# One encoder layer on one core: the first norm's scale and shift in four column blocks, and four weight units multiplied row block by row block

## The reference, cut to what matters

```python
mod = silu(c) @ w_ada + b_ada                      # 9 vectors of 1024
sh1, sc1, g1, sh2, sc2, g2, sh3, sc3, g3 = split(mod, 9)
h = rms_norm(x, ffn1_norm) * (1 + sc1) + sh1
x = x + 0.5 * g1 * ((silu(h @ w1) * (h @ w3)) @ w2)   # w1, w3: 1024x2816
```

## Time and profile before

| what | value |
|---|---|
| median of 3 runs | 1123.41 us (1123.1 to 1124.43) |
| profiled execution: span | 1122.3 us, mean granted TensorE clock 0.981; the page gives no other time of it |
| busy | PE 95%, DVE 54%, ACT 36%, POOL 15% |
| upper part of a unit, ACT L358 | x168, mean 1059 ns |
| lower part of a unit, DVE L673 | x166, mean 1261 ns |
| modulation product, DVE L697 | x54, mean 1347 ns |
| gate product, DVE L741 | x44, mean 688 ns |
| first norm's reciprocal and diagonal, DVE L708, L710 | 0.18 and 0.69 us |
| HBM read | 129.85 MB, 118 GB/s over the span |

### The profile page before, as it was taken

How to read it: one execution, slowest core, us unless ns; L and a number is a source line. 1 busy time by engine, 2 the same in 40 slices (tenths; PEclk the granted TensorE clock), 3 DMA queues, 4 the chain that set the end, 5 groups by cost and what they waited for, 6 DMA issues and landing times.

```text
span 1122.3 us, 13691 instructions
## 1 busy us (share of the span) xinstructions
PE 1066.8 (95%) x4902; PEld 873.7 (78%) x4902; DVE 606.9 (54%) x700; ACT 404.6 (36%) x516; POOL 163.9 (15%) x149
## 2 busy tenths in 40 slices
PE   3899999999999999998998888999999999999997
PEld 3788888888888888786776767778888888888885
DVE  5877677633342326659899899553333333322324
ACT  3242222222311223575865665343232222222211
POOL 2211111000000101016382533010000000000100
PEclk9799999999999999998999899999999999999999
DMA  8678788622222223221111111213322223222222
GB/s 300 230 246 278 262 264 262 203 91 97 94 94 93 94 94 139 78 82 49 56 57 57 51 43 39 76 57 108 98 93 93 93 95 105 98 94 94 93 94 75
DMA packets 37393, 132.41 MB, mean 118 GB/s; under 512 B 4080, under 2 KB 4336, under 8 KB 37232
## 3 DMA queue, kind: packets, MB, share of 16 engines
q1 hardware_dynamic: 28992, 100.83, 26.7%
q0 software_dynamic: 8368, 31.13, 8.2%
HBM read 129.85 MB, written 2.10 MB: 118 GB/s over the span
## 4 chain that ended last, share of the span: by engine, by line
PE 83%; DVE 10%; issue 3%; DMA 2%; ACT 2%; SPq 0%; DVEq 0%; ACTq 0%
PE psum L1127 25%; PE psum L1129 24%; PE psum L1128 24%; PE psum L1362 2%; PE psum L1376 1%; DVE qk L976 1%; DMA ada<-wada 1%; PE psum L1332 1%; DVE qk L975 1%; PE psum L1164 1%; DVE acc L697 1%; DMA raw<-wu 1%; DVE wlo L673 1%; PE psum L1233 1%; PE psum L1303 1%
## 5 line engine op out<-in xcount | busy, mean ns | idle before, releaser
L673 DVE TENSOR_TENSOR wlo<-raw,whi 128x1024 fp32r<-128x1024 f32 x166 | 209.3, 1261 | 340.9 <-ACT whi L358 340.7
L358 ACT ACTIVATE whi<-raw 128x1024 fp32r<-128x1024 f32 x168 | 177.9, 1059 | 563.6 <-PE psum L1129 549.0
L1127 PE MATMUL psum<-hhi,whi 128*128 128x512 f32 x896 | 359.6, 401 | 10.5 <-DVE sg L927 5.4
L1128 PE MATMUL psum<-hlo,whi 128*128 128x512 f32 x896 | 351.9, 393 | 0.0
L1129 PE MATMUL psum<-hhi,wlo 128*128 128x512 f32 x896 | 351.6, 392 | 0.0
L1127 PEld LDWEIGHTS psum<-hhi,whi 128*128 128x128 f32 x896 | 170.3, 190 | 50.9 <-DVE wlo L673 7.7
L1129 PEld LDWEIGHTS psum<-hhi,wlo 128*128 128x128 f32 x896 | 170.1, 190 | 36.3
L1128 PEld LDWEIGHTS psum<-hlo,whi 128*128 128x128 f32 x896 | 170.4, 190 | 35.4 <-issue 1.9
L1127 PE MATMUL psum<-ghi,whi 128*128 (+1 forms) x352 | 138.5, 394 | 0.0
L1129 PE MATMUL psum<-ghi,wlo 128*128 (+1 forms) x352 | 138.1, 392 | 0.0
L1128 PE MATMUL psum<-glo,whi 128*128 (+1 forms) x352 | 136.8, 389 | 0.0
(11 more groups left out here) (172 smaller groups left out, 970.7 us busy)
## 6 DMA issues: line engine op xcount, KB each, us to landing
raw<-wu SPq DMA_DIRECT2D x168, 512.0 KB, 3.3
ada<-wada POOLq DMA_DIRECT2D x56, 512.0 KB, 5.0
ada<-wada SPq DMA_DIRECT2D x16, 512.0 KB, 4.7
x<-xt SPq DMA_DIRECT2D x2, 1024.0 KB, 10.2
out<-outt SPq DMA_DIRECT2D x8, 256.0 KB, 2.2
bd<-bd POOLq DMA_DIRECT2D x1, 1024.0 KB, 5.1
dif<-consts POOLq DMA_DIRECT2D x1, 448.0 KB, 6.1
resets<-consts POOLq DMA_DIRECT2D x1, 256.0 KB, 6.9
```

What stands on the lines that cost most here:

```text
L358: nc.scalar.activation(whi[:, slot, :], raw[:, slot, :], ACT.Copy).then_inc(hi_done, 1)
L673: nc.vector.tensor_tensor(wlo[:, slot, :], raw[:, slot, :], whi[:, slot, :], ALU.subtract).then_inc(lo_done, 1)
L1127: nc.tensor.matmul(dst, a, rhi, start=start, stop=False)
L1128: nc.tensor.matmul(dst, a, rlo, start=False, stop=False)
```

## The change

The first 16 modulation tiles are laid out anew in memory, in four blocks: block q holds, for both sc1 and sh1, the 256 columns that belong to row blocks 2q and 2q+1; a row of it is 512 wide (256 of each), and it comes as four tiles of 512 KB that hold two k each. All four blocks have their own place (`early`), in the room that the FFN's product takes later, and so have units 2 and 3 (`raw2`, `whi2`, `wlo2`), so SyncE issues all these loads without a wait: x in quarters, block 0, units 0 and 1, block 1, units 2 and 3, blocks 2 and 3.

Of each block's 8 products `ON_PE` says how many TensorE makes itself, as four single-column matmuls with cs as the moving column (4, 2, 2, 0 for the blocks); the other 24 in all stay on VectorE at half width, and TensorE adds their sum over the partitions to the same PSUM columns (`block_sums`). The squares of x lie in eight buffers and are summed on VectorE, not on GpSimd. The scale and shift columns come per block (`block_columns`), and the rows of h two by two. Rows 0 to 3 are made as before; for rows 4 to 7 GpSimd multiplies x by the norm's broadcast (copied to SBUF by ScalarE, `rbs`), and ScalarE makes both the upper part and the full value, with scale and shift. GpSimd makes the lower parts of four units instead of two. TensorE multiplies units 0 to 3 in pieces of row blocks, in the order of the list below. Units 4 and 5 take the two old slots after it; the third modulation vector is summed one pair of units later than before, and so are those after it. The two exponentials of the mixer go to the start of the first down projection.

```diff
--- before.py
+++ after.py
+BLOCKS = 4
+ON_PE = (4, 2, 2, 0)
...
+        early, off = at("early", [P, BLOCKS, KD, T], F32, off)
+        raw2, off = at("raw2", [P, 2, UNIT], F32, off)
+        whi2, off = at("whi2", [P, 2, UNIT], F32R, off)
+        wlo2, off = at("wlo2", [P, 2, UNIT], F32R, off)
...
+        sq0, _ = at("sq0", [P, KD, T], F32, off)
...
@@ SyncE @@
-            for k in range(4):
-                sp_.dma_start(ada[:, k, :], wada[k]).then_inc(ada_first[k], 16)
-            for i in range(2):
-                n = KD // 2
-                sp_.dma_start(x[:, n * i:n * i + n, :], xt[T * i:T * i + T].rearrange("(d p) t -> p d t", p=P)
-                              ).then_inc(x_loaded, 16)
-            for k in range(4, 16):
-                sp_.wait_ge(ada_added, k - 3)
-                sp_.dma_start(ada[:, k % 4, :], wada[k]).then_inc(ada_first[k % 4], 16)
-            for u in range(2):
-                sp_.dma_start(raw[:, u, :], wu[u]).then_inc(raw_loaded[u], 16)
-            with sp_.Fori(1, N_UNITS // 2) as j:
+            for i in range(4):
+                n = KD // 4
+                sp_.dma_start(x[:, n * i:n * i + n, :], xt[n * P * i:n * P * i + n * P].rearrange("(d p) t -> p d t", p=P)
+                              ).then_inc(x_loaded[i], 16)
+            for q in range(BLOCKS):
+                for i in range(4):
+                    n = 4 * q + i
+                    sp_.dma_start(early[:, q, 2 * i:2 * i + 2, :].rearrange("p k c -> p (k c)"), wada[n]
+                                  ).then_inc(first_loaded[n], 16)
+                if q < 2:
+                    for u in range(2):
+                        sp_.dma_start((raw, raw2)[q][:, u, :], wu[2 * q + u]
+                                      ).then_inc((raw_loaded, extra_loaded)[q][u], 16)
+            with sp_.Fori(2, N_UNITS // 2) as j:
...
@@ GpSimd @@
-            add_squares(0, 0)
-            add_squares(0, 1)
+            def lower(u, raw, up, low):
+                pool.wait_ge(hi_done, u + 1)
+                nc.gpsimd.tensor_tensor(low[:, u % 2, :], raw[:, u % 2, :], up[:, u % 2, :], ALU.subtract
+                                        ).then_inc(lo_done, 1)
+            def x_rooted(d):
+                nc.gpsimd.tensor_tensor(xr[:, d - 4, :], x[:, d, :], rbs[:], ALU.mult).then_inc(xr_done, 1)
+            for u in range(2):
+                lower(u, raw, whi, wlo)
+            pool.wait_ge(rb_copied, 1)
+            x_rooted(4)
+            x_rooted(5)
+            for u in range(2, 4):
+                lower(u, raw2, whi2, wlo2)
+            x_rooted(6)
+            x_rooted(7)
+            pool.wait_ge(sq_added, 4)
+            pool.wait_ge(first_loaded[-1], 16)
             for k in range(8):
-                pool.wait_ge(ada_added, 13 + k)
+                if k >= 4:
+                    pool.wait_ge(ada_added, k - 3)
                 pool.dma_start(ada[:, k % 4, :], wada[16 + k]).then_inc(ada_loaded[k % 4], 16)
...
@@ ScalarE @@
+            def first_square(d):
+                act.wait_ge(x_loaded[d // 2], 16)
+                nc.scalar.activation(sq0[:, d, :], x[:, d, :], ACT.Square).then_inc(sq_done, 1)
+            def hi_extra(slot):
+                act.wait_ge(extra_loaded[slot], 16)
+                nc.scalar.activation(whi2[:, slot, :], raw2[:, slot, :], ACT.Copy).then_inc(hi_done, 1)
+            def first_h(d):
+                q = d // 2
+                if d < 4:
+                    act.wait_ge(block_ready, 2 * q + 1)
+                    act.wait_ge(htmp_done, d + 1)
+                    nc.scalar.activation(hhi[:, d, :], tmp[:, d % 2, :], ACT.Identity, bias=mod("sh1", d)
+                                         ).then_inc(hhi_done, 1)
+                else:
+                    act.wait_ge(block_ready, 2 * q + 2)
+                    act.wait_ge(xr_done, d - 3)
+                    nc.scalar.activation(hhi[:, d, :], xr[:, d - 4, :], ACT.Identity, bias=mod("sh1", d),
+                                         scale=scale[:, d:d + 1]).then_inc(hhi_done, 1)
+                    act.wait_ge(hlo_done, d - 1)
+                    nc.scalar.activation(tmp[:, d % 2, :], xr[:, d - 4, :], ACT.Identity, bias=mod("sh1", d),
+                                         scale=scale[:, d:d + 1]).then_inc(htmp_done, 1)
...
+                if n == 0:
+                    act.wait_ge(small_done, 1)
+                    nc.scalar.activation(small[:, 32:40], small[:, 32:40], ACT.Exp).then_inc(cs_done, 1)
+                    nc.scalar.activation(small[:, 40:56], small[:, 40:56], ACT.Exp).then_inc(cs_done, 1)
...
-                square(0, d)
+                first_square(d)
             act.wait_ge(ones_set, 2)
             root(0)
             hi(0, 0)
+            first_h(0)
             hi(0, 1)
-            h_upper(0)
+            first_h(1)
+            act.wait_ge(htmp_done, 2)
+            nc.scalar.activation(rbs[:], rb(0), ACT.Copy).then_inc(rb_copied, 1)
+            hi_extra(0)
+            hi_extra(1)
+            for d in range(2, KD):
+                first_h(d)
...
@@ VectorE @@
+            def add_first_squares(i):
+                dve.wait_ge(sq_done, 4 * i + 4)
+                a = 4 * i
+                nc.vector.tensor_tensor(sq0[:, a:a + 2, :], sq0[:, a:a + 2, :], sq0[:, a + 2:a + 4, :], ALU.add
+                                        ).then_inc(sq_added, 1)
+                dve.wait_ge(sq_added, 2 * i + 1)
+                nc.vector.tensor_tensor(sq0[:, a, :], sq0[:, a, :], sq0[:, a + 1, :], ALU.add).then_inc(sq_added, 1)
+            def block_add(q, k):
+                n = sum(KD - ON_PE[i] for i in range(q)) + k - ON_PE[q]
+                half = slice(T * (q % 2), T * (q % 2) + T)
+                dve.wait_ge(first_loaded[4 * q + k // 2], 16)
+                dst = acc[:, half]
+                if k == KD - 1:
+                    dst = fin[:, half]
+                    if q >= 2:
+                        dve.wait_ge(block_summed, q - 1)
+                if k == ON_PE[q]:
+                    if q >= 2:
+                        dve.wait_ge(first_added, n)
+                    nc.vector.tensor_scalar(dst, early[:, q, k, :], cs[:, k:k + 1], None, ALU.mult).then_inc(first_added, 1)
+                else:
+                    dve.wait_ge(first_added, n)
+                    nc.vector.scalar_tensor_tensor(dst, early[:, q, k, :], cs[:, k:k + 1], acc[:, half], ALU.mult,
+                                                   ALU.add).then_inc(first_added, 1)
+            def block_columns(q):
+                dve.wait_ge(block_summed, q + 1)
+                nc.vector.tensor_tensor(of_block(mods, q), modq(q).rearrange("p (m d) -> p m d", m=2),
+                                        of_block(vecs[:, VEC["b_ada"]:VEC["b_ada"] + 2 * KD], q), ALU.add
+                                        ).then_inc(block_ready, 1)
+                dve.wait_ge(block_ready, 2 * q + 1)
+                d = 2 * q
+                nc.vector.scalar_tensor_tensor(scale[:, d:d + 2], mod("sc1", d, 2), 1.0, vec("norm0", d, 2), ALU.add,
+                                               ALU.mult).then_inc(block_ready, 1)
+            def first_tmp(d):
+                dve.wait_ge(block_ready, 2 * (d // 2) + 2)
+                if d >= 2:
+                    dve.wait_ge(hlo_done, d - 1)
+                    dve.wait_ge(rb_copied, 1)
+                nc.vector.scalar_tensor_tensor(tmp[:, d % 2, :], x[:, d, :], scale[:, d:d + 1],
+                                               rb(0) if d < 2 else rbs[:], ALU.mult,
+                                               ALU.mult).then_inc(htmp_done, 1)
+            def first_lower(d):
+                dve.wait_ge(hhi_done, d + 1)
+                if d < 4:
+                    nc.vector.scalar_tensor_tensor(hlo[:, d, :], tmp[:, d % 2, :], mod("sh1", d), hhi[:, d, :], ALU.add,
+                                                   ALU.subtract).then_inc(hlo_done, 1)
+                else:
+                    dve.wait_ge(htmp_done, d + 1)
+                    nc.vector.tensor_tensor(hlo[:, d, :], tmp[:, d % 2, :], hhi[:, d, :], ALU.subtract
+                                            ).then_inc(hlo_done, 1)
...
+            add_first_squares(0)
             dve.wait_ge(cs_done, 1)
-            for k in range(8):
-                ada_add(0, k)
-            for k in range(8):
-                ada_add(1, k)
-                if k == 3:
-                    mod_bias(0)
-                if k == 4:
-                    rms_inverse(0, rms_done, rinv_done, diag_done)
-            dve.wait_ge(mod_ready, 1)
-            nc.vector.scalar_tensor_tensor(scale[:, 0:KD], mod("sc1", 0, KD), 1.0, vec("norm0", 0, KD), ALU.add,
-                                           ALU.mult).then_inc(cols_ready, 1)
-            h_split(0)
+            block_add(0, 4)
+            add_first_squares(1)
+            for k in range(5, KD):
+                block_add(0, k)
+            rms_inverse(0, rms_done, rinv_done, diag_done)
```

(131 more changed lines are left out.)

80 lines of the change are left out of this document (38 added, 42 removed).

## The result

The changed kernel takes **1131.49 us** (median of 4 runs, 1130.49 to 1133.85) against 1123.89 for the kernel before beside it: ratio 1.0070, 95% interval 1.0057 to 1.0082. It is slower by 0.7%. The profiled execution took 1130.49 us, with a span of 1128.7, 6.4 more than before. Two executions of later kernels, of 1622.6 and 2177.3 us, lie far from all others and are left out of their kernels' medians and ratios.

A forecast was written before the change was run, and what follows sets the result against it. TensorE, busy 95% of the span, was taken as the bound, with time to win only where it waits or runs slow. Unit 4 starting 6.1 us later gave 1123.4 + 6.1 = 1129.5 us; own range 1126 to 1133, whole range 1119 to 1135.5.

The forecast's parts named there:

- Transfers hidden: Opening loads, issued without waits: blocks 1 to 3 land by 23.4, 31.3 and 36.5 us, before VectorE needs them, costing nothing.
- The rival of late early work: Unit 0 or 1 arrives late in the opening, costing up to 3 us: 1132 us; chance 0.04.
- Opening: From x's squares to row 1's lower half: done at 28.4 us instead of 47.5, 19 us won.
- Block 1: VectorE's six products take turns with six GpSimd operations, 12.3 us to 40.7; rows 2 and 3 done at 46.1.
- Block 2: Sums wait behind two direct products and 24 matmuls on TensorE: columns at 54.1 us, rows 4 and 5 at 57.6.
- Block 3: All eight products on VectorE until 63.6 us, lower-clock sums and columns 65.9, last row 69.4, 14 us later than before.
- Rest: TensorE's 36 matmuls after block 3's sums, then ScalarE's silu chain: unit 4, the mark, starts at 76.9 us, 5.2 later.
- Clock: Rises of TensorE's clock at other moments put unit 4 at 76.4 to 81 us; 77.8 taken, 6.1 later than before.
- TensorE keeps the upper clock: Rival: early work holds TensorE's clock up through the opening and blocks, unit 4 at 70.3, time 1122.0 us; chance 0.12.
- At nothing: Moved exponentials with a 1.28 us table load, under 2 us of ScalarE, fit a 2.63 us idle gap at no cost.
- The sum: Whole kernel: 1123.4 us plus 6.1 for unit 4's later start gives 1129.5 us.
- Nothing different after: Sign of being right: the profile after unit 4's start, from 76 to 81 us, looks as before, adding 0 us.

The follow-up runs named there:

- the second profile: The changed kernel run again unaltered, against the kernel before: 1132.77 us, ratio 1.0077, unit 4 at 78.61 us.
- its mends: Changed kernel with blocks 1-3's running sums in PSUM, block 2's sums before unit 2's matmuls, rows 2 and 3 reading the norm from PSUM: 1124.89 us, ratio 0.9997.

## Why the prediction was right

1. *Transfers hidden.* Right. Block 0's third tile (products 4 and 5) is in use at 13.63, forecast 14.2, and no later product waited for data. The rival of late early work is out.
2. *Opening.* Forecast 18.8 for block 0's products, 19.2 for its sums, 24.3 for two products with the norm, 28.4 for row 1. Measured 18.34, 19.13, 24.2 and 28.30. The sums ran at the lower clock, as taken (1.71 for eight matmuls).
3. *Block 1.* Forecast 12.3 us of taking turns, ending at 40.7; measured 12.0, ending at 40.25. Shown to be GpSimd's doing by its short operations (5.3) and by the sum in PSUM (5.0). Sums 1.8 forecast, 1.87 measured; rows 2 and 3 forecast for 46.1, done at 45.6.
4. *Block 2.* Columns forecast for 54.1, done at 53.8; TensorE's queue was the cause, shown by the sums put first. Rows 4 and 5 at 57.6, measured 57.5.
5. *Block 3.* Products 63.6, columns 65.9, last row 69.4; measured 63.9, 66.3 and 70.0. Of the small miss 0.3 was there when the products ended; most of the rest is ScalarE's operation with scale and bias: 0.80, where I had taken 0.7.
6. *Rest.* I forecast unit 4 at 76.9 with a table load of 1.28 behind unit 0. Measured 76.56, but by other terms: the load came at 69.23, while unit 0 was still at work, so it cost nothing and silu began at 71.58 and not 72.5; then the gate product at 72.94 waited for unit 1, which I hadn't counted, and from silu to unit 4 it took 4.98 and not 4.4.
7. *Clock.* I had added 0.9 for rises at other moments. The first profile needed none of it, the second 1.7 (78.61). The **TensorE keeps the upper clock** rival is out: the granted clock was 0.50 from 17.6 to 24.4, from 31.2 to 48.3 and from 61.9 to 68.8. Single-column matmuls ran at the upper clock from 12.1 on, and it fell just ahead of block 0's sums (19.13). One price was right for another reason than mine: the clock fell at 31.2, 2.3 us before TensorE came to rest (33.5), while I had put the lower clock of block 1's sums down to that rest. In the second profile it fell within the rest, at 37.5. That the forecast fits the first profile here is luck. From 25 to 31 the clock was 1.00, where I had drawn on the 0.50 of before: it rose at 24.4, in fillers behind the two 512-column matmuls of the norm's broadcast, and in the second profile only at 27.2. The Trainium skill, TensorE: Matmul & The Clock Gate, section "What's actually happening", sets the clock by how busy the engine has been. Taken as the profile's busy share, that isn't the full account here: TensorE was busy 6.70 of 6.70 us from 17.9 to 24.6 at 0.52, and 3.30 of 3.30 from 42.9 to 46.2 at 0.50.
8. *At nothing.* Right. The exponentials stand between two table loads of 1.28 each, from 308.70 to 311.61, where I had named one load, and the next ScalarE copy still had 1.00 us of idle time before it.
9. *The sum.* I forecast 6.1 later; the medians say 7.6, the profiled spans 6.4. The term that was mis-sized is the one after unit 4, where I had put nothing: the mark itself came 4.9 later in the first profile and 7.0 later in the second, and the mixer added 1.4 and 1.7. "Nothing different after" was one of my signs of being right, and it did not hold. In the fourteen profiles of this case the mixer took between 313.8 and 318.1 us, whatever the edit. That the lower clock lay over other matmuls there is seen in the lines above; why it fell where it did wasn't tried and stays open. The marks of the two profiles lie on either side of the forecast 77.8, so the way to unit 4 is borne out; the mixer's 1.4 and 1.7 were not in the forecast at all.

## What to carry to other kernels

Before work is split into earlier pieces, ask which engine's operations will then lie beside each other: six VectorE products of 0.48 to 0.75 us took 12 us beside six GpSimd operations, because both engines read SBUF and took turns. A running sum that lives in PSUM takes VectorE out of this, for 0.26 us more at a block's first product. In the kernel before, this edit alone gained 0.1 to 0.2%; the whole reordering, with its mends, gained nothing that the totals can tell. And work that arrives early in one queue delays whatever sums stand behind it: put short producers ahead of long consumers, and move no more to an engine than it can do before it is asked for it.

## What the runs showed of the hardware that I had not expected

- The granted clock can fall while TensorE does single-column matmuls without a pause. It fell to 0.50 at 17.6 in the changed kernel, with TensorE busy since 6.4, and within the sums behind 32 direct matmuls in all three kernels that had these (67.1, 58.8 and 61.8). Behind 16 direct matmuls in the same place it stayed at 1.00.
- Fillers ahead of single-column work helped in one of two places: the clock stayed at 1.00 over block 3's sums (1.05 us) and the unit matmuls behind them, but fell within block 1's sums (1.42 us), and the 16 direct matmuls behind these took 3.55 us, as without fillers.
- A product with its running sum in PSUM runs beside GpSimd at full width too: 128x1024 over two banks in 1.29 us, as in SBUF undisturbed. Only the single-input form is slower with PSUM as its target, 0.74 instead of 0.48 for 128x512 and 1.29 instead of 0.75 for 128x1024.
- An early gain of 4.5 us can be gone by the end: the mixer, the same code in every kernel, differed by up to 4.3 us. A stretch of 3.2 us at the lower clock cost nothing where idle time followed its matmuls (before, at 608.4), and 1.7 us where none did (after, at 621.8). A profile's mark near the edit tells more of the edit than the total.
